# Order of the matmuls in a half unit: the token half becomes the outer loop, so that 24 matmuls (12 in a down tile) in a row accumulate in one PSUM bank

## What is computed

```
u = rmsnorm(x) ;  proj = u @ w_in            # 2048 -> 6752: q, k, v, indexer, z, x/B/C, dt
att = sparse attention over top-k keys       # prompt, and cached keys for the samples
y   = Mamba-2 scan, gated, normalised
h = x + concat(att, y) @ w_out               # 2048 -> 2048
f = rmsnorm(h)
h = h + (silu(f @ w_gate) * (f @ w_up)) @ w_down   # 2048 -> 5632 -> 2048
out = rmsnorm(h)
```

## Time and profile before

| what | value |
|---|---|
| median of 3 runs | 3274.39 us |
| runs | 3269.07 to 3275.76 us |
| profiled execution, its own time | 3267.44 us |
| span of its instructions | 3265.6 us |
| mean granted TensorE clock | 0.956 |

### The profile page before, as it was taken

The page is one execution under the profiler, slowest core; times in us unless marked ns, Lnnn a source line. Parts: engine busy times, 40 slices in busy tenths (PEclk is TensorE's granted clock), DMA queues, the critical chain, the costliest instruction groups (busy, mean ns, idle before and its releaser), DMA issues.

```text
span 3265.6 us, 53293 instructions
## 1 busy us (share of the span) xinstructions
PE 3057.1 (94%) x21743; PEld 2899.3 (89%) x21743; DVE 957.0 (29%) x1714; ACT 763.0 (23%) x1171; POOL 981.5 (30%) x406
## 2 busy tenths in 40 slices
PE   6999997899999996899999999999999999999997
PEld 6887996687777784899999999999999999999997
DVE  2322797434333432212221221221212121121223
ACT  4223222222222222223212121212121112112122
POOL 2322332111111110233333333333333333333331
PEclk8999998998889996899999999999999999999998
DMA  6322223444444443432222222222222222222221
GB/s 186 109 66 72 92 92 91 115 131 139 129 126 117 115 126 114 139 100 93 78 78 86 96 78 78 78 84 98 78 78 78 86 96 78 78 78 89 93 91 59
DMA packets 350273, 317.78 MB, mean 97 GB/s; under 512 B 39821, under 2 KB 319413, under 8 KB 348808
## 3 DMA queue, kind: packets, MB, share of 16 engines
q1 hardware_dynamic: 319368, 293.93, 29.0%
q10 hardware_dynamic: 30720, 21.05, 2.1%
HBM read 284.90 MB, written 31.43 MB: 97 GB/s over the span
## 4 chain that ended last, share of the span: by engine, by line
PE 57%; issue 34%; POOL 7%; ACTq 1%; DVE 1%; ACT 0%; POOLq 0%; DVEq 0%
PE G L705 40%; PE G L1117 17%; POOL WL L634 4%; POOL WL L663 3%; ACTq L1167 0%; ACTq L1168 0%; DVE us L2016 0%; DVE y_out L2035 0%; POOL WL L655 0%; ACT WRAW L1176 0%; PE B L720 0%; ACTq L39 0%; DVE gs L1987 0%; ACT XR L1181 0%; DVE hl L2022 0%
## 5 line engine op out<-in xcount | busy, mean ns | idle before, releaser
L705 PE MATMUL G<-AH,WH 128*128 128x288 f32 (+1 forms) x5024 | 1090.4, 299 | 42.0 <-DVE us L2016 12.2
L705 PE MATMUL G<-AL,WH 128*128 128x288 f32 (+1 forms) x5024 | 1077.9, 296 | 0.0
L705 PE MATMUL G<-AH,WL 128*128 128x288 f32 (+1 forms) x5024 | 1076.5, 296 | 0.0
L705 PEld LDWEIGHTS G<-AH,WH 128*128 128x128 f32 (+1 forms) x5024 | 814.2, 191 | 69.4 <-issue 51.3
L705 PEld LDWEIGHTS G<-AL,WH 128*128 128x128 f32 (+1 forms) x5024 | 814.9, 190 | 0.0
L705 PEld LDWEIGHTS G<-AH,WL 128*128 128x128 f32 (+1 forms) x5024 | 813.4, 190 | 0.0
L655 POOL TENSOR_TENSOR WL<-WRAW,WH 128x1024 fp32r<-128x1024 f32 x208 | 517.4, 2488 | 943.6 <-ACT WH L648 943.6
L648 ACT CAST WH<-WRAW 128x1024 fp32r<-128x1024 f32 x208 | 218.5, 1051 | 1006.6 <-PE G L705 900.1
L653 POOL TENSOR_TENSOR WL<-WRAW,WH 128x1024 fp32r<-128x1024 f32 x88 | 210.8, 2395 | 357.9 <-ACT WH L646 357.9
L1117 PE MATMUL G<-hh,WH 128*128 128x288 f32 x1408 | 303.0, 296 | 4.6 <-DVE hl L2022 4.6
L1117 PE MATMUL G<-hl,WH 128*128 128x288 f32 x1408 | 300.3, 294 | 0.0
(11 more groups left out here) (308 smaller groups left out, 2018.9 us busy)
## 6 DMA issues: line engine op xcount, KB each, us to landing
WRAW<-in_w_gate SPq DMA_DIRECT2D x22, 2048.0 KB
WRAW<-in_w_up SPq DMA_DIRECT2D x22, 2048.0 KB
WRAW<-in_w_down SPq DMA_DIRECT2D x22, 2048.0 KB
WRAW<-in_w_in SPq DMA_DIRECT2D x14, 2048.0 KB, 8.6
raw<-in_w_in SPq DMA_DIRECT2D x48, 512.0 KB, 4.0
kca<-in_cache_k SPq DMA_DIRECT2D x256, 64.0 KB, 2.0
vca<-in_cache_v SPq DMA_DIRECT2D x256, 64.0 KB, 2.0
WRAW<-in_w_out SPq DMA_DIRECT2D x16, 1024.0 KB
```

Of the source, the lines that this page charges most:

```text
L705: last = nc.tensor.matmul(G[gslot][0:width, h, 0:HALF], wt[:, half, k % 8, 0:width], act[:, (k + shift) % KT, h * HALF:(h + 1) * HALF], st ...
```

## The change

In `half_unit` and in `down_half` the loop over the token halves, which was the innermost, is made the outermost. The same matmuls are issued, each with its weight load, but all those of half 0 first and then all those of half 1. `ready(k)` is called on the pass over half 0 alone.

```diff
             pe.wait_ge(s["w_lo"], c + 1)
-            for k in range(8 * half, 8 * half + 8):
-                if ready:
-                    ready(k)
-                for wt, act in ((WH, AH), (WH, AL), (WL, AH)):
-                    for h in range(2):
+            for h in range(2):
+                for k in range(8 * half, 8 * half + 8):
+                    if ready and h == 0:
+                        ready(k)
+                    for wt, act in ((WH, AH), (WH, AL), (WL, AH)):
                         last = nc.tensor.matmul(G[gslot][0:width, h, 0:HALF], wt[:, half, k % 8, 0:width], act[:, (k + shift) % KT, h * HALF:(h + 1) * HALF],
...
                     pe.wait_ge(s["tile_taken"], T + t - 1)
-                    for k in range(4):
-                        for wt, act in ((WH, hh), (WH, hl), (WL, hh)):
-                            for h in range(2):
+                    for h in range(2):
+                        for k in range(4):
+                            for wt, act in ((WH, hh), (WH, hl), (WL, hh)):
```

## The result

| | before | changed |
|---|---|---|
| median, 8 runs each | 3271.08 us | 3285.17 us |
| range of runs | 3268.34 to 3275.76 | 3281.66 to 3291.31 |
| span of the profiled execution | 3265.6 us | 3289.5 us |

The ratio is 1.0042, with a 95% interval from 1.0031 to 1.0053: 14.1 us slower, 10 to 17 by the interval. The profiled execution of before, 3267.44 us, is quicker than all eight runs, and that of the changed kernel, 3291.31, is the slowest of its eight, so their spans are 24 us apart and not 14; what follows goes by rows within stretches, not by the spans.

A forecast was written before the change was run, and what follows sets the result against it. The prediction took TensorE's row of matmuls as the bound; distance 0, paced tiles 2.0 and `rest` 0 gave +2.0 us on 3267.4, so 3269.4 us (3276.4 on the median), range 3235 to 3303.

The forecast's parts named there:

- TensorE's row of matmuls is the bound: Whole kernel: TensorE busy 3057.1 of 3265.6 us, 19,296 matmuls before and after; unchanged parts cost nothing by themselves.
- The distance: Time between matmul starts on lines 705 and 1117, mean 132.1 ns: change taken as 0; each ns worth 19.3 us.
- The bounds: All matmuls of lines 705 and 1117 in one rhythm: 40.0 us less if quick, 23.7 us more if slow.
- The first rival: Gate and up stretches behind down tiles lose the quick rhythm, all matmuls slow: +25.7 us, 3300 us; chance 0.20.
- only part is lost: Only part of the 5760 quick matmuls lose their rhythm, or a down tile grows: slower, chance 0.10.
- The second rival: All matmuls of lines 705 and 1117 in the quick rhythm: -38.0 us, 3238 us; chance 0.20.
- The paced tiles: First tiles of output projection (+1.5 us, 1.0 to 3.6), FFN (0.1) and input projection (+0.4): together 2.0 us.
- `rest` at 0: Last half unit of each turn, eight times: `rest` starts 1.6 us sooner, put at 0; at most 12.8 us.
- The sum: Whole kernel: 0 + 2.0 + 0 = +2.0 us, giving 3269.4 us, or 3276.4 on the median.
- A write to the bank just written waits: Matmuls repeating one bank: from 3 ns more each, +58 us, 3334 us; chance 0.02.
- the cost falls to that of line 1076: Every matmul: 5 ns over the columns in place of 12, -135 us, 3141 us; chance 0.03.
- alternation costs clock: Matmuls in the turns: changing banks lowers the clock, one bank gives back up to 26 us, 3250 us; chance 0.01.

The follow-up runs named there:

- e5: Kernel before, operand order kept, but the bank changes only with step k (six matmuls in a row to one bank; sums wrong): 3272.03 us, one execution.
- e6: Changed kernel, operand order kept, but the bank changes at every matmul (sums wrong): 3283.00 us, one execution.
- e7: Kernel before with the new order, except in down tiles, gate and up tiles behind them, and half units calling `ready(k)`: 3268.58 us, ratio 0.9989.
- e1: Kernel before with the new order in `down_half` alone; `half_unit` keeps the old order: 3294.47 us, ratio 1.0068.
- e8: Kernel before, old order, but token half 1 ahead of half 0 in each pair, in both functions: 3281.12 us, one execution.
- e4: Kernel before with the new order only in half units that take `ready(k)`: 3274.51 us, ratio 1.0005.
- e3: Changed kernel with the old order kept in half units that take `ready(k)`: 3283.83 us, ratio 1.0036 against the kernel before.
- e10: Changed kernel with the pass over token half 1 first: 3291.21 us, one execution.
- e11: Changed kernel with both passes reading the columns of token half 0, so half 1 repeats half 0: 3280.99 us, one execution.
- e2: Kernel before with the new order in `half_unit` alone; `down_half` keeps the old order: 3281.95 us, ratio 1.0028.

## Why the prediction was right or wrong

The time lay in the range, because its two ends were the two rhythms; but the expected +2.0 us was 14.1, and the greatest chance, 0.40, was on a quicker kernel. That the range held is no proof of the account: the term that decides the case was put at nothing. Point by point:

- *TensorE's row of matmuls is the bound, nothing is removed or added, the other engines keep their places.* Right: the chain is the same kind of row, and every us that was found is one of distance between starts, of a paced tile, or of a wait behind the 576.
- *The distance, "I take 0, by the rows at which the code is now, because nothing in the rows ties either rhythm to the bank".* This is the step that failed. The premise was right, as e5 and e6 show: the bank is nothing. But the change moves operands too, and the step spoke of the bank alone. Two rhythms under one code and one use of the banks said only that the bank does not choose between them; they were no ground to put the change of distance at nothing. The new order has one distance of its own, 132.5 ns, so the 5760 quick matmuls lost theirs: 10 x 1.44 = 14.4 us. The down tiles added 10 x 0.2 = 2.0. The slow ones won: 0.7 us on the 912, 9 x 0.14 = 1.3 on the 192 ahead of the later down tiles, and 1.2 on the 1440 (191.05 in e7 against 192.23 in e5). Together +13.2.
- *The bounds, 40.0 us less and 23.7 more.* They held, and the time fell between them. They do not give the sign: only once the one distance is known to be 132.5 ns does it follow, as 5760 x 2.5 ns lost against at most 9312 x 0.8 won, of which part is at half clock.
- *The first rival, all in the slow rhythm, with "only part is lost".* Its mechanism, that another order of down matmuls may spoil how TensorE comes into the 576, is what e1 shows by itself, and at its full price, +22 us. In the changed kernel it has nothing left to act on, since the order behind the down tiles has only one distance. So the case that came was the partial one, at more than half of the bound.
- *The second rival, all in the quick rhythm.* Not seen in the changed kernel. In e8 and e4 single stretches do change to it, by the entry and not by the bank.
- *The paced tiles, +1.5 of 1.0 to 3.6 at the output projection.* 1.7 against before, 2.0 against e3, and the wait for GpSimd was gone as said. The path was only in part as said: the pass over half 1 took 4.37 us in place of 3.2, since half of it ran at half clock (1.2 us more, where 2.6 was put as the most), and the second half unit was not held by the last step of the low part. The first tile of the FFN took 16.1 us before and after, that of the input projection 16.8 and 17.1, near the 0.1 and 0.4 forecast. *`rest` at 0* was neither shown nor refuted.
- *The sum.* The waits behind the 576 give some of the 13.2 back (1.35 us in place of 1.52 at the first, 1.8 us over the nine inside the loop), and by the spans 11.2 are left from the second tile of the output projection on. With 1.7 for the first tile that is 12.9 us against 14.1 measured (10 to 17). What the change does ahead of the output projection, `rest` included, is lost in the several us by which that part varies.
- *A write to the bank just written waits; the cost falls to that of line 1076; alternation costs clock.* None of the three is seen: e5 writes one bank six times in a row at the distances of before, no row comes near the second, and for the third the clock is 1.00 in the long stretches of both orders.

## What to carry to other kernels

In a long row of matmuls without a wait, measure the distance between starts stretch by stretch before changing the order: a few ns per matmul is the whole effect, and two stretches of the same code can differ. When a loop is turned round, list every thing that is turned with it; here it was named for its banks, and only the columns and weights that follow each other counted. The new order had one distance wherever it stood, but not the quickest, and a gain in one stretch has to be looked for in the stretch behind it too, because the order ahead can take it away.

## What the runs showed of the hardware

- The same instructions in the same order ran in one of two steady rhythms, 130.0 or 133.3 ns for 288 columns at the full clock, for 75 to 190 us on end. Behind the down tiles which one depended on the matmuls ahead (74.89 against 76.81 us for 576, e1; the fourfold table above), in all ten stretches of a run; elsewhere it also differed with the same matmuls ahead (12.80 us for the last tile of the input projection before, 12.48 in e1). Why there are two is not known.
- How often the bank changed made no difference: 74.89 us for 576 with a change at each matmul (before) or at each sixth (e5), and 76.33 with a change at each 24th (the changed kernel) or at each (e6).
- Which 288 of the 576 columns were read made 1.6 ns per matmul: 131.7 for the first, 133.3 for the second half of `AH` and `AL` (e10, e11). With `hh` and `hl` the first half was the slow one, 133.3 against the mean of 132.8 over both.
- At the full clock all distances (130.0 to 133.4 ns) lay above the 120.0 ns of the columns. The Trainium skill, TensorE: Matmul & The Clock Gate, section on the back-to-back issue gap, gives columns / 2.4 + 2.5 ns, which would be 122.5 here, as the gap of a single isolated matmul, and says that in a stream with a weight load for each the spacing is set by both; no run here came near 122.5.
- Two executions of the same program reached the end of the input projection 7.3 us apart (517.48 us in the changed kernel's, 510.22 in e2's), at a granted clock of 0.97 against 0.99 between 320 and 520 us.
